# One layer of a hybrid mixer and expert kernel: loads in order of use, a first piece of three tiles, and early splits of the last head's output made sooner

## The chip, the cores and the metric

The kernel runs on one core of one Trainium2 chip, in one launch. The metric is the device time of that launch in microseconds, taken as the median of several runs. Before the change three runs gave 1456.88, 1457.09 and 1457.78 us, so the median is 1457.09 us.

## The reference

A layer with 16 meta rows ahead of 1024 tokens, so 1040 rows of width 1024, all in float32:

```
h   = concat(meta, x)                            # 1040 x 1024
xn  = rms_norm(h, mix_norm_w)
proj = xn @ w_in                                 # 28 column tiles of 128, and 8 columns for a, b
y_a = rms_norm_by_64(gate_b * conv3(gate_c * u))
q, k, v = silu(conv4(qkv)); q, k l2-normalised
o   = gated_delta_rule(q, k, v, g, beta)         # 4 heads of 128, chunks of rows
y_b = rms_norm(o) * silu(z)
h   = h + concat(y_a, y_b) @ w_out
h   = h + experts(rms_norm(h, ffn_norm_w))       # 32 experts, 2 per token
out = rms_norm(h, final_norm_w)[16:]
```

## The kernel before

**Split products.** Each float32 matrix that TensorE multiplies is split in two: a high part, which ScalarE makes by copying into a reduced format, and a low part, which VectorE makes as the value less its high part. A product is then three matmuls (high by high, high by low, low by high), the three lines 1132 to 1134 in `project` and the lines 441 to 443 in `out_product`.

**The start.** The 1040 rows are ten tiles of C = 104 rows. A tile is loaded by the SyncE queue (`load_x`, line 1086), squared, summed and turned into a scale by ScalarE (`token_norm`, lines 1390 to 1398), multiplied by that scale and by the norm weight `mixrow` on VectorE (line 1581), transposed in eight blocks by TensorE (`turn_x`, line 1157), and split (high part ScalarE line 1403, low part VectorE line 1587). The 1040 columns of `xn_hi` and `xn_lo` that result are handed to `project` in the three pieces of `PIECE`: 348, 346 and 346 columns. The first nine units of projection are three pieces by three weight tiles (Q, K, V of head 0); unit n works on piece n // 3. The weight tiles `p_raw` are loaded by the same SyncE queue (`load_p`, line 1091), split by `hi_part` (line 1374) and `lo_part` (line 1572).

The SyncE queue issues row tiles 0 to 3, then the three weight tiles, then row tiles 4 to 9. The ScalarE queue issues first the small constants, then 104 copies of the norm weight, the parameters and the rest of the constants. TensorE transposes tiles 0 to 3, then does unit 0, and one more tile's transpose ahead of each unit. ScalarE keeps tile t+2's norm ahead of tile t-1's high part. ScalarE evacuates each unit (`first_piece`, line 1384) and VectorE convolves each evacuated unit (four instructions, lines 1624 and 1622), after all low parts and after the low part of the small weight `wab` (line 1594). Then come the products with `wab` (line 1179), the projection of Z for head 0, which needs a weight tile whose low part VectorE makes after the nine convolutions, and the gates.

**The heads.** Heads 0 to 2 run in a loop, head 3 (`last`) is unrolled behind it. A head solves a triangular system in rounds: `z` (line 1254), `rz` (line 1252), and `ttr` (line 1250) on TensorE, each in three groups that go to banks 3 to 5; VectorE takes `z` (line 1691) and `rz` (line 1689) out, ScalarE `ttr` (line 1482). Projection units, called fills, are put between the rounds; in head 3 they are used up after the round rz2. Then follows a scan over ten chunks.

**The early output product.** In head 3 the output weight is split too: ScalarE `w_out_hi` (line 1525) in three parts after ttr3, ttr4 and ttr5, GpSimd `w_out_lo` (line 1878). The first three blocks of 128 rows of the output product take six of their eight weight tiles (`EARLY`) as fills of the scan. Their left operand is split by `early_high` on ScalarE (line 1488) and `early_low` on VectorE (line 1761). `early_high(0)`, `(1)`, `(2)` stand behind the three parts of the `w_out_hi` split; `early_low` stands behind rz3, rz4 and rz5 in VectorE's order. Block u's split lies where the weight slot u of the projection was: slot 1 held GC, slot 2 UU, slot 0 GB.

Of the kernel before, what the change touches and what calls it, by code (L numbers as in the profile page):

```python
# [21 lines left out]
F32 = mybir.dt.float32  # L22
I32 = mybir.dt.int32
F32R = mybir.dt.float32r
ALU = mybir.AluOpType
# [7 lines left out]
C = 104  # L33
# [5 lines left out]
PIECE = [(0, 348), (348, 346), (694, 346)]  # L39
# [72 lines left out]
def layer_kernel(nc, x, consts, par, mix_w, wt, w_out, ffn_w, fin_w, w_gate, w_up, w_down, out):  # L112
    ctx = ExitStack()
    with ctx:  # L114
# [144 lines left out]
        x_loaded = [sem(f"token_rows_loaded{s}") for s in range(NC)]  # L259
# [464 lines left out]
        def tail_vector(dve):  # L724
# [247 lines left out]
            for t in range(FT + 1):  # L972
                if t < FT:
                    dve.wait_ge(hf_loaded[t], 32)
# [107 lines left out]
        def _(sp):  # L1082
            def load_x(t):
                if t >= NX:
                    sp.wait_ge(xn_done, t - NX + 1)
                sp.dma_start(x_sb[t % NX][0:C, :], x[t * C:(t + 1) * C, :]).then_inc(x_loaded[t], 16)
# [6 lines left out]
            for t in range(4):  # L1093
                load_x(t)
            for n, s in enumerate((1, 2, 0)):
                load_p(s, n)
            for t in range(4, NC):
                load_x(t)
# [49 lines left out]
        def _(pe):  # L1148
# [216 lines left out]
        def _(act):  # L1365
            act.dma_start(const_sb[:, 0:NFIRST], consts[:, 0:NFIRST]).then_inc(s_first, 16)
            act.dma_start(mixrow[0:C, :], mix_w[0:C, :]).then_inc(s_mix, 16)
            act.dma_start(par_sb, par).then_inc(s_const, 16)
            act.dma_start(const_sb[:, NFIRST:NCONST], consts[:, NFIRST:NCONST]).then_inc(s_const, 16)
# [16 lines left out]
            def token_norm(t):  # L1386
                act.wait_ge(x_loaded[t], 16)
# [19 lines left out]
            for t in range(NC + 1):  # L1407
                for tt in (range(3) if t == 0 else range(t + 2, min(t + 3, NC))):
                    token_norm(tt)
                if t:  # L1410
                    xn_high(t - 1)
                if t in (2, 3, 4):
                    hi_part((1, 2, 0)[t - 2], 1)
                if t == 5:
                    act.wait_ge(s_const, 32)
                    nc.scalar.activation(wab_hl[:, :, 0:8], wab, ACT.Copy).then_inc(wab_done, 1)
                if t >= 6:
                    if t == 6:
                        act.wait_ge(zeros_done, 3)
                    first_piece(t - 6)  # L1420
            for n in range(5, 9):
                first_piece(n)
# [67 lines left out]
            def mixer(h, last):  # L1490
# [25 lines left out]
                for n in range(1, LEVELS - 1):  # L1516
                    grp(h, f"ttr{n}", tI)
                    if not last and n in (3, 5):
                        kind = Q if n == 3 else K
                        hi_part(SLOT[kind], use(h, kind))  # L1520
                    if last and n >= 3:
# [4 lines left out]
                        early_high(n - 3)  # L1526
# [39 lines left out]
        def _(dve):  # L1566
            for u in range(3):
# [7 lines left out]
            dve.wait_ge(s_mix, 16)  # L1575
            for t in range(NC + 1):
                if t < NC:
                    dve.wait_ge(rstd_done, t + 1)
                    if t >= NB:
                        dve.wait_ge(xt_done, 2 * (t - NB + 1))  # L1580
                    nc.vector.scalar_tensor_tensor(xn_sb[t % NB][0:C, :], x_sb[t % NX][0:C, :], nstat[0:C, 2, t:t + 1],
                                                   mixrow[0:C, :], ALU.mult, ALU.mult).then_inc(xn_done, 1)
                if t:
                    for b in range(2):
                        dve.wait_ge(xhi_done, 2 * (t - 1) + b + 1)
                        cols = slice((t - 1) * C, t * C)
                        nc.vector.tensor_tensor(xn_lo[:, 4 * b:4 * b + 4, cols],
                                                bank[3 + 2 * ((t - 1) % 2) + b][:, 0:4 * C].rearrange("p (k c) -> p k c", k=4),
                                                xn_hi[:, 4 * b:4 * b + 4, cols].bitcast(F32),
                                                ALU.subtract).then_inc(xlo_done, 1)  # L1590
                if t in (2, 3, 4):
                    lo_part((1, 2, 0)[t - 2], 1)
# [102 lines left out]
            def mixer(h, last):  # L1695
# [60 lines left out]
                def early_low(t):  # L1756
# [3 lines left out]
                    dve.wait_ge(ye_hi, t + 1)  # L1760
# [3 lines left out]
                if last:  # L1764
# [182 lines left out]
```

## Time and profile before

| what | value |
|---|---|
| median of three runs | 1457.09 us |
| the profiled execution | 1456.85 us |
| its span | 1455.0 us |
| TensorE busy | 1291.5 us, 89% |
| TensorE weight loads | 1138.4 us, 78% |
| VectorE busy | 918.7 us, 63% |
| ScalarE busy | 719.6 us, 49% |
| GpSimd busy | 162.7 us, 11% |
| mean granted TensorE clock | 0.946 |

Between the span and the time of the execution lie 1.85 us. The granted clock is a share of full speed: 1.00 is 2.4 GHz and 0.50 is 1.2 GHz; a stretch between the two was partly at each. An instruction's row gives its start and its duration; durations of matmuls overlap, so what one costs is the distance from its start to the next start. The number in brackets is how long the engine was idle ahead of the row, with what ended that.

### The profile page before, as it was taken

The numbers are of one execution on the slowest core, as the hardware profiler recorded it, in microseconds if no ns is written. First come the engines' busy times: TensorE is split into PE (matmuls) and PEld (weight loads), VectorE is DVE, ScalarE is ACT, GpSimd is POOL, SyncE is SP. The second block draws the span as 40 slices with busy tenths as digits, with TensorE's granted clock in tenths as the row PEclk, the third lists the DMA queues.
The fourth block names the chain that finished last, engine by engine and source line by source line (L and its number), as shares of the span: only waits on it lengthen the run. The fifth ranks groups of instructions, "written<-read, shape, count | busy, mean of one in ns | idle before, by whom it ended". The sixth has DMA issues, their size and how long they took to land. (4 is left out here: it accounts for less than half of the span.)

```text
span 1455.0 us, 20112 instructions
## 1 busy us (share of the span) xinstructions
PE 1291.5 (89%) x7434; PEld 1138.4 (78%) x7434; DVE 918.7 (63%) x1138; ACT 719.6 (49%) x920; POOL 162.7 (11%) x143
## 2 busy tenths in 40 slices
PE   3999998999899989789995599999999999999950
PEld 2989997999799989767885488888888888888840
DVE  4654555445445463433315688888888888888827
ACT  6251234123412341233312477777777877777723
POOL 0010111011101120420000311111111111111000
PEclk9999999999999999889995799999999999999985
DMA  7000111010001010305510799999999999999848
GB/s 201 30 30 16 30 30 30 15 30 30 30 15 30 29 30 1 116 0 201 190 60 28 271 350 369 372 373 382 382 384 378 383 377 375 378 378 374 316 175 345
DMA packets 38163, 274.01 MB, mean 188 GB/s; under 512 B 8159, under 2 KB 8415, under 8 KB 25815
## 3 DMA queue, kind: packets, MB, share of 16 engines
q1 hardware_dynamic: 28050, 250.69, 46.1%
q0 software_dynamic: 9216, 16.80, 3.0%
q10 hardware_dynamic: 837, 5.65, 1.1%
q8 instruction: 46, 0.75, 0.2%
q14 instruction: 14, 0.11, 0.0%
HBM read 260.52 MB, written 29.36 MB: 199 GB/s over the span
## 5 line engine op out<-in xcount | busy, mean ns | idle before, releaser
L787 DVE TENSOR_TENSOR w_lo<-w_raw,w_hi 128x2048 fp32r<-128x2048 f32 x192 | 433.4, 2286 | 67.7 <-ACT w_hi L642 67.7
L642 ACT ACTIVATE w_hi<-w_raw 128x2048 fp32r<-128x2048 f32 x192 | 357.1, 1916 | 18.5 <-PE bank L524 13.8
L1132 PE MATMUL bank<-xn_hi,p_hi 128*128 128x346 f32 (+1 forms) x672 | 231.9, 345 | 0.0
L1133 PE MATMUL bank<-xn_lo,p_hi 128*128 128x346 f32 (+1 forms) x672 | 219.9, 327 | 0.0
L1134 PE MATMUL bank<-xn_hi,p_lo 128*128 128x346 f32 (+1 forms) x672 | 219.1, 326 | 0.0
L522 PE MATMUL bank<-w_hi,xgT_hi 128*128 128x512 f32 x512 | 206.5, 403 | 2.9 <-DVE xgT_lo L911 2.9
L524 PE MATMUL bank<-w_hi,xgT_lo 128*128 128x512 f32 x512 | 200.8, 392 | 0.0
L523 PE MATMUL bank<-w_lo,xgT_hi 128*128 128x512 f32 x512 | 200.5, 392 | 0.0
L1132 PEld LDWEIGHTS bank<-xn_hi,p_hi 128*128 128x128 f32 x672 | 130.4, 194 | 0.4
L1133 PEld LDWEIGHTS bank<-xn_lo,p_hi 128*128 128x128 f32 x672 | 130.2, 194 | 0.3
L1134 PEld LDWEIGHTS bank<-xn_hi,p_lo 128*128 128x128 f32 x672 | 129.3, 192 | 0.0
L522 PEld LDWEIGHTS bank<-w_hi,xgT_hi 128*128 128x128 f32 x512 | 97.0, 189 | 21.6 <-issue 3.6
L524 PEld LDWEIGHTS bank<-w_hi,xgT_lo 128*128 128x128 f32 x512 | 96.7, 189 | 20.8
L523 PEld LDWEIGHTS bank<-w_lo,xgT_hi 128*128 128x128 f32 x512 | 97.1, 190 | 18.4
L1482 ACT ACTIVATE arena<-bank 104x416 f32<-104x416 f32 (+1 forms) x72 | 28.4, 459 | 158.2 <-PE bank L1250 158.1
L522 PE MATMUL bank<-w_hi,hidT_hi 128*128 128x512 f32 x256 | 100.7, 393 | 3.0 <-DVE hidT_lo L922 3.0
L524 PE MATMUL bank<-w_hi,hidT_lo 128*128 128x512 f32 x256 | 100.3, 392 | 0.0
L523 PE MATMUL bank<-w_lo,hidT_hi 128*128 128x512 f32 x256 | 100.2, 391 | 0.0
L996 POOL DMA_INDIRECT y_rows<-arena x32 | 32.2, 1006 | 504.9 <-ACT arena L673 504.9
L1822 DVE SCALAR_TENSOR_TENSOR arena<-arena,bank 128x128 f32<-128x128 f32 x40 | 13.9, 347 | 86.3 <-PE bank L1292 86.3
L673 ACT ACTIVATE arena<-bank,arena 128x512 f32<-128x512 f32 x64 | 40.5, 685 | 52.0 <-PE bank L524 52.0
L1378 ACT ACTIVATE arena<-bank 128x346 f32<-128x346 f32 (+1 forms) x39 | 18.0, 461 | 95.7 <-PE bank L1134 95.6
(233 smaller groups left out, 2050.9 us busy)
## 6 DMA issues: line engine op xcount, KB each, us to landing
w_raw<-in_w_down SPq DMA_DIRECT2D x32, 2048.0 KB, 9.8
w_raw<-in_w_gate SPq DMA_DIRECT2D x31, 2048.0 KB, 10.4
w_raw<-in_w_up SPq DMA_DIRECT2D x31, 2048.0 KB, 9.5
p_raw<-in_w_tiles SPq DMA_DIRECT2D x28, 512.0 KB, 3.6
arena<-y_rows SPq DMA_DIRECT2D x8, 1024.0 KB, 12.0
arena<-in_tokens SPq DMA_DIRECT2D x10, 416.0 KB
w_out_raw<-in_w_out SPq DMA_DIRECT2D x4, 1024.0 KB, 8.6
arena<-in_tokens SPq DMA_DIRECT2D x8, 512.0 KB, 4.2
```

Source lines behind the costliest of these rows:

```text
L522: nc.tensor.matmul(out, xh, wh, start=start, stop=False)
L523: nc.tensor.matmul(out, xh, wl, start=False, stop=False)
L524: return nc.tensor.matmul(out, xl, wh, start=False, stop=stop_)
L642: nc.scalar.activation(w_hi[m][:, half], wraw[m][:, half], ACT.Copy).then_inc(hi_done[m], 1)
L673: m = nc.scalar.activation(ysb[p][:, b * 512:(b + 1) * 512], bank[3 + b][:, :], ACT.Copy, scale=wcol[p])
L787: nc.vector.tensor_tensor(w_lo[m][:, half], wraw[m][:, half], w_hi[m][:, half].bitcast(F32), ALU.subtract).then_inc(lo_done[m], 1)
L996: nc.gpsimd.indirect_dma_start(out=y_dram, out_offset=bass.IndirectOffsetOnAxis(ap=si[p], axis=0), in_=ysb[p], in_offset=None, bounds_chec ...
L1132: nc.tensor.matmul(out[:, 0:n], p_hi[slot][:, k, :], hi, start=(k == 0), stop=False)
L1133: nc.tensor.matmul(out[:, 0:n], p_hi[slot][:, k, :], lo, start=False, stop=False)
L1134: m = nc.tensor.matmul(out[:, 0:n], p_lo[slot][:, k, :], hi, start=False, stop=(k == KD - 1))
L1378: nc.scalar.activation(raw[buf][:, 3 + o:3 + o + n], bank[pc][:, 0:n], ACT.Copy).then_inc(proj_act, 1)
L1482: nc.scalar.activation(dst[0:C, gsl(g), :], bmat(g)[0:C], ACT.Copy).then_inc(gdn_act, 1)
```

## The change

Three things are changed together.

1. **Loads.** The norm weight is loaded as one row, first on the SyncE queue; TensorE spreads it over the partitions by a product with a row of ones, and VectorE copies it out of two banks into `mixrow`. Row tiles 0 to 3 follow, then weight tile, row tile 4, weight tile, row tile 5, weight tile, row tile 6 and on. The parameters and the remaining constants come last on that queue; the ScalarE queue only issues the small constants. Row loads share eight semaphores.
2. **Pieces.** `PIECE` is 312, 364 and 364 columns, so piece 0 needs three row tiles, piece 1 seven and piece 2 ten. TensorE transposes tiles 0 to 2, then tile 3 ahead of unit 0, tile 4 ahead of unit 1, tiles 5 and 6 ahead of unit 2, and 7, 8, 9 ahead of units 3, 4, 5. ScalarE and VectorE are reordered to match; the split of `wab` now stands behind the evacuation of unit 5.
3. **Last head.** `early_high(1)` moves behind ttr1, `early_high(2)` and `(0)` behind ttr2, `early_low(1)` behind rz2, `early_low(2)` and `(0)` behind rz3.

```diff
-PIECE = [(0, 348), (348, 346), (694, 346)]
+PIECE = [(0, 3 * C), (3 * C, 364), (3 * C + 364, 364)]
+READY = [-(-(o + n) // C) for o, n in PIECE]
@@ sync
-            for t in range(4):
-                load_x(t)
-            for n, s in enumerate((1, 2, 0)):
-                load_p(s, n)
-            for t in range(4, NC):
-                load_x(t)
+            sp.dma_start(xn_sb[NB - 1][0:1, :], mix_w[0:1, :]).then_inc(s_mix, 16)
+            for t in range(NC):
+                load_x(t)
+                if t in (3, 4, 5):
+                    load_p((1, 2, 0)[t - 3], t - 3)
+            sp.dma_start(par_sb, par).then_inc(s_const, 16)
+            sp.dma_start(const_sb[:, NFIRST:NCONST], consts[:, NFIRST:NCONST]).then_inc(s_const, 16)
@@ tensor
-            for t in range(4):
+            pe.wait_ge(s_mix, 16)
+            pe.wait_ge(mix_one, 1)
+            for b in range(2):
+                nc.tensor.matmul(bank[b][0:C, 0:512], r_sb[0:1, 0:C], xn_sb[NB - 1][0:1, b * 512:(b + 1) * 512],
+                                 start=True, stop=True).then_inc(mix_ps, 1)
+            for t in range(3):
                 turn_x(t)
             for n in range(9):
                 pc, s = n // 3, n % 3
-                if n + 4 < NC:
-                    turn_x(n + 4)
-                pe.wait_ge(xlo_done, 2 * (4, 7, 10)[pc])
+                for t in ((3,), (4,), (5, 6), (7,), (8,), (9,))[n] if n < 6 else ():
+                    turn_x(t)
+                pe.wait_ge(xlo_done, 2 * READY[pc])
@@ early_unit
-                if k == 0 and b == 0:
-                    pe.wait_ge(ye_lo, t + 1)
+                if n == 0:
+                    pe.wait_ge(ye_lo, 3)
@@ scalar
-            for t in range(NC + 1):
...
+            for t in range(3):
+                token_norm(t)
+            for t in range(NC):
+                xn_high(t)
+                if t == 0:
+                    hi_part(1, 1)
+                if t == 2:
+                    token_norm(3)
+                    hi_part(2, 1)
+                if t >= 2 and t + 2 < NC:
+                    token_norm(t + 2)
+                if t == 3:
+                    hi_part(0, 1)
+                    act.wait_ge(zeros_done, 3)
+                if t >= 4:
+                    first_piece(t - 4)
+            act.wait_ge(s_const, 32)
+            nc.scalar.activation(wab_hl[:, :, 0:8], wab, ACT.Copy).then_inc(wab_done, 1)
+            for n in range(6, 9):
                 first_piece(n)
@@ scalar, mixer
+                    if last and n == 1:
+                        early_high(1)
+                    if last and n == 2:
+                        act.wait_ge(proj_done, tile_done(h, GB))
+                        early_high(2)
+                        early_high(0)
...
-                        early_high(n - 3)
@@ vector (scale and low part in ScalarE's order)
+            for t in range(3):
+                token_scale(t)
+            for t in range(NC):
+                xn_low(t)
+                if t == 0:
+                    lo_part(1, 1)
+                if t == 2:
+                    token_scale(3)
+                    lo_part(2, 1)
+                if t >= 2 and t + 2 < NC:
+                    token_scale(t + 2)
+                if t == 3:
+                    lo_part(0, 1)
@@ vector, mixer
                     grp(h, "rz2")
+                    early_low(1)
                     mix_conv()
...
                         grp(h, f"rz{n}")
-                        early_low(n - 3)
+                        if n == 3:
+                            early_low(2)
+                            early_low(0)
...
-                    if last and n == 5:
-                        early_low(2)
```

## Rows read from the trace of the kernel before

**Rows 1.** First part of the page: busy time of each engine.
```profile
PE 1291.5 (89%) x7434; PEld 1138.4 (78%) x7434; DVE 918.7 (63%) x1138; ACT 719.6 (49%) x920; POOL 162.7 (11%) x143
```

**Rows 2.** Timeline, 0 to 35: start, duration (us), instruction, [idle before, releaser].
```profile
5.08 1.06 ACT L1390 ACTIVATE arena<-arena 104x1024 f32<-104x1024 f32 x1 [0.83 <-DMA arena<-in_tokens]
6.66 0.20 ACT L1398 ACTIVATE arena<-arena 104x1 f32<-104x1 f32 x1
10.07 2.48 DVE L1581 SCALAR_TENSOR_TENSOR arena<-arena 104x1024 f32<-104x1024 f32 x2 [9.15 <-DMA arena<-in_mix_w]
...
17.14 1.09 DVE L1587 TENSOR_TENSOR xn_lo<-bank,xn_hi 128x416 fp32r<-128x416 f32 x2 [4.59 <-ACT xn_hi L1403]
21.76 1.06 ACT L1390 ACTIVATE arena<-arena 104x1024 f32<-104x1024 f32 x1 [4.25 <-DMA arena<-in_tokens]
24.17 1.06 ACT L1374 ACTIVATE p_hi<-p_raw 128x1024 fp32r<-128x1024 f32 x1
31.09 1.65 PE L1157 MATMUL bank<-arena 104*128 104x104 f32 x8 [1.71 <-DVE arena L1581]
32.43 0.64 PE L1132 MATMUL bank<-xn_hi,p_hi 128*128 128x348 f32 x1
```

**Rows 3.** Windows: stretch, length, engines' busy time, granted clock, DMA share, GB/s.
```profile
15.00:19.00 4.00, 0.00 (x0) 0.00 (x0) 1.86 (x3) 2.45 (x6) 0.00 (x0) 1.00 0.83 339
20.00:30.00 10.00, 2.77 (x15) 2.13 (x13) 5.83 (x8) 8.05 (x18) 0.00 (x0) 1.00 0.84 204
```

**Rows 4.** Timeline, 58 to 80, the end of the first nine units.
```profile
58.54 0.17 DVE L1612 COPY arena<-arena 128x16 f32<-128x16 f32 x1
61.06 0.46 ACT L1384 ACTIVATE arena<-bank 128x346 f32<-128x346 f32 x1 [2.92 <-PE bank L1134]
64.86 0.46 ACT L1384 ACTIVATE arena<-bank 128x346 f32<-128x346 f32 x1 [3.34 <-PE bank L1134]
76.46 1.81 DVE L1622 SCALAR_TENSOR_TENSOR arena<-arena 128x346 f32<-128x346 f32 x3
78.19 1.22 DVE L1572 TENSOR_TENSOR p_lo<-p_raw,p_hi 128x1024 fp32r<-128x1024 f32 x1
79.88 0.32 PE L1132 MATMUL bank<-xn_hi,p_hi 128*128 128x348 f32 x1
```

**Rows 5.** Timeline of TensorE at the start of head 1.
```profile
238.30 3.83 PE L1234 MATMUL bank<-arena 104*128 104x416 f32 x6 [4.61 <-issue]
```

**Rows 6.** TensorE behind an idle stretch (timeline), and three windows with their granted clock.
```profile
551.39 3.58 PE L1254 MATMUL bank<-arena 104*104 104x104 f32 x20 [1.95 <-ACT arena L1482]
311.00:323.00 12.00, 11.86 (x110) 10.66 (x108) 7.02 (x13) 7.15 (x12) 4.52 (x2) 1.00 0.16 45
551.00:555.00 4.00, 3.61 (x21) 3.61 (x22) 1.43 (x3) 0.98 (x3) 0.00 (x0) 0.58 0.00 0
603.70:609.70 6.00, 5.95 (x34) 5.95 (x35) 2.33 (x5) 1.25 (x4) 1.71 (x1) 0.50 0.14 53
```

**Rows 7.** Timeline of the last head's rounds.
```profile
592.50 0.52 DVE L1743 TENSOR_TENSOR arena<-bank,arena 128x346 f32<-128x346 f32 x1 [2.79 <-PE bank L1134]
595.34 2.00 PE L1252 MATMUL bank<-arena 104*104 104x104 f32 x20
596.27 1.60 DVE L1689 TENSOR_TENSOR arena<-arena,bank 104x416 f32<-104x416 f32 x3 [0.23 <-PE bank L1252]
601.66 1.53 DVE L1761 TENSOR_TENSOR y_lo<-arena,y_hi 128x768 fp32r<-128x768 f32 x1 [3.78 <-ACT y_hi L1488]
603.75 3.80 PE L1252 MATMUL bank<-arena 104*104 104x104 f32 x20 [3.37 <-DVE arena L1691]
613.32 2.89 DVE L1761 TENSOR_TENSOR y_lo<-arena,y_hi 128x768 fp32r<-128x768 f32 x1 [5.36 <-ACT y_hi L1488]
616.77 3.80 PE L1252 MATMUL bank<-arena 104*104 104x104 f32 x20 [5.40 <-DVE arena L1691]
629.80 3.50 PE L1252 MATMUL bank<-arena 104*104 104x104 f32 x20 [3.32 <-DVE arena L1691]
```

More of the change, by code:

```diff
@@ L38 @@
 Z, GC, UU, GB, Q, K, V = range(KINDS)
-PIECE = [(0, 348), (348, 346), (694, 346)]
+PIECE = [(0, 3 * C), (3 * C, 364), (3 * C + 364, 364)]
+READY = [-(-(o + n) // C) for o, n in PIECE]
+NXS = 8
 LEVELS = 7
@@ L258, in layer_kernel @@
         s_wout = [sem(f"w_out_loaded{i}") for i in range(4)]
-        x_loaded = [sem(f"token_rows_loaded{s}") for s in range(NC)]
+        x_loaded = [sem(f"token_rows_loaded{s}") for s in range(NXS)]
+        mix_one, mix_ps, mix_done = sem("mix_ones_set"), sem("mix_in_psum"), sem("mix_rows_done")
         s_mix, wab_done, abt_done = sem("mix_row_loaded"), sem("wab_done"), sem("abt_done")
@@ L973, in tail_vector @@
                 if t < FT:
-                    dve.wait_ge(hf_loaded[t], 32)
+                    dve.wait_ge(hf_loaded[t], 48 if t + NXS < NC else 32)
                     dve.wait_ge(yf_loaded[t], 16)
@@ L1085, in load_x @@
                     sp.wait_ge(xn_done, t - NX + 1)
-                sp.dma_start(x_sb[t % NX][0:C, :], x[t * C:(t + 1) * C, :]).then_inc(x_loaded[t], 16)
+                sp.dma_start(x_sb[t % NX][0:C, :], x[t * C:(t + 1) * C, :]).then_inc(x_loaded[t % NXS], 16)
             def load_p(s, n):
@@ L1366, in _ @@
             act.dma_start(const_sb[:, 0:NFIRST], consts[:, 0:NFIRST]).then_inc(s_first, 16)
-            act.dma_start(mixrow[0:C, :], mix_w[0:C, :]).then_inc(s_mix, 16)
-            act.dma_start(par_sb, par).then_inc(s_const, 16)
-            act.dma_start(const_sb[:, NFIRST:NCONST], consts[:, NFIRST:NCONST]).then_inc(s_const, 16)
             nc.scalar.preload_act_table_set("natural_log_exp_and_others")
@@ L1386, in token_norm @@
             def token_norm(t):
-                act.wait_ge(x_loaded[t], 16)
+                act.wait_ge(x_loaded[t % NXS], (t // NXS + 1) * 16)
                 if t:
@@ L1405, in xn_high @@
                                          ACT.Copy).then_inc(xhi_done, 1)
-            for t in range(NC + 1):
[L1408 to L1421, printed above, removed]
+            for t in range(3):
[17 more added lines that the diff above has]
+            for n in range(6, 9):
                 first_piece(n)
@@ L1566, in _ @@
         def _(dve):
+            nc.vector.memset(r_sb[0:1, :], 1.0).then_inc(mix_one, 1)
             for u in range(3):
@@ L1573, in lo_part @@
                                         ALU.subtract).then_inc(p_lo_done[slot], 1)
[L1575 to L1592, printed above, removed]
@@ new lines, in _, with token_scale @@
+            for b in range(2):
+                dve.wait_ge(mix_ps, b + 1)
+                nc.vector.tensor_copy(mixrow[0:C, b * 512:(b + 1) * 512], bank[b][0:C, 0:512]).then_inc(mix_done, 1)
+            dve.wait_ge(mix_done, 2)
+            def token_scale(t):
+                dve.wait_ge(rstd_done, t + 1)
+                if t >= NB:
+                    dve.wait_ge(xt_done, 2 * (t - NB + 1))
+                nc.vector.scalar_tensor_tensor(xn_sb[t % NB][0:C, :], x_sb[t % NX][0:C, :], nstat[0:C, 2, t:t + 1],
+                                               mixrow[0:C, :], ALU.mult, ALU.mult).then_inc(xn_done, 1)
@@ new lines, in xn_low @@
+            def xn_low(t):
+                cols = slice(t * C, (t + 1) * C)
+                for b in range(2):
+                    dve.wait_ge(xhi_done, 2 * t + b + 1)
+                    nc.vector.tensor_tensor(xn_lo[:, 4 * b:4 * b + 4, cols],
+                                            bank[3 + 2 * (t % 2) + b][:, 0:4 * C].rearrange("p (k c) -> p k c", k=4),
+                                            xn_hi[:, 4 * b:4 * b + 4, cols].bitcast(F32), ALU.subtract).then_inc(xlo_done, 1)
+            for t in range(3):
+                token_scale(t)
@@ L1759, in early_low @@
                             for a in (y_lo[t], yT[:, :, META + t * 128:META + (t + 1) * 128], y_hi[t].bitcast(F32))]
-                    dve.wait_ge(ye_hi, t + 1)
+                    dve.wait_ge(ye_hi, (3, 1, 2)[t])
                     nc.vector.tensor_tensor(part[0], part[1], part[2], ALU.subtract).then_inc(ye_lo, 1)
```

## The prediction

> **What bounds the kernel now.** I read the page's first part first: TensorE is busy for 89% of the span [rows 1], so time can come only from stretches where it waits, or runs at the lower of its two clock levels. The timeline shows the reader the first such stretch. TensorE's steady work starts with the transposes of tile 3 at 31.09 and unit 0 at 32.43. Ahead of it ScalarE sits idle for 4.25 us, until row tile 4 is there at 21.76, because three weight tiles stand before that tile in the queue, and it takes up the first weight tile only at 24.17; VectorE waits until 10.07 for the norm weight [rows 2]. Windows say what the loads can give: 339 GB/s while weight tiles move, 204 GB/s with row tiles alone [rows 3]. The timeline from 58 to 80 shows who comes next: VectorE convolves without a pause from 58.71 to 78.27 and ends the low part of the Z tile at 79.41, and TensorE takes it at 79.88 [rows 4]. So VectorE has 0.5 us of slack there. Last, the rounds of the last head: TensorE waits 3.37, 5.40 and 3.32 us at `rz4`, `rz5` and `rz6` for VectorE's `z` evacuation, and VectorE itself had stood behind `early_low`, which waited 3.78 and 5.36 us for ScalarE [rows 7]. Each wait is followed by a round at the lower clock: `rz` takes 3.80, 3.80 and 3.50 us there, against 2.00 before [rows 7].
>
> **Part 1, the loads.** A row tile of 426 KB takes 2.08 us at 204 GB/s, a weight tile of 524 KB takes 1.55 us at 339 GB/s [rows 3]. Tile 0 is used at 5.08 [rows 2], and as the norm weight's 426 KB and the parameters no longer run beside it, I leave it there. Then tiles 1 to 3 are usable at 7.2, 9.2 and 11.3, the first weight tile at 12.9, tile 4 at 15.0, and with two more weight tiles between, tile 9 at 28.5. The parameters and constants (0.94 MB) end near 32, and their first users are the splits of `wab` near 50. They cost nothing. SyncE's queue waits for freed buffers only at tiles 7 to 9, of which the first three scalings, done near 13.6, are the condition.
>
> The norm weight now needs two 512-column products. The nearest row is 3.83 us for 1040 columns at the lower clock [rows 5], so 3.8 us; with small constants there at about 5.3 and a copy of 0.6 (an estimate from 1.09 for two of 416 [rows 2]) it is ready near 9.8, where it was 10.07. Its bounds are 7.5 (upper clock) and 10.5; both lie hidden, as the next step waits for the weight tile.
>
> The chain on ScalarE, with 1.78 for a norm (5.08 to 6.86), 1.24 for a scaling, 1.65 for a tile's transposes, about 1.0 for its high part and 1.06 for a weight's [rows 2]: norms 0 to 2 end at 11.0; tile 0 is scaled at 11.1, turned at 12.8, its high part ends at 13.3, the weight's at 14.3, tile 1's at 15.2. Tile 2's transposes need tile 0's low part (14.6), so its high part ends at 16.9, norm 3 at 18.6, scaling 3 at 19.9. Piece 0 would be ready near 18, but tile 3's transposes stand ahead of unit 0 in TensorE's order; they start at 20.0, where they started at 31.09. That is 11.1 us earlier, and from there TensorE has the same list in sum (the same transposes, the same 1040 columns), with tile 9 in place long before piece 2 needs it.
>
> So the `wab` products would end at 68.8 instead of 79.9. **What is late next** is VectorE. Its convolutions used to start as soon as the last low part was done, ahead of unit 5's end (ScalarE evacuates it at 61.06 [rows 4]). Now the `wab` split stands behind that evacuation on ScalarE, and VectorE waits for it, with all nine convolutions queued behind the wait and the Z tile's low part behind those. Unit 5 ends at 60.95 less 11.1, less 0.6 for 18 columns that went from pieces 0 and 1 to piece 2 (72 matmuls at 0.458 ns a column, from 3.80 us for a unit [rows 4]): 49.3. Evacuation and the small splits bring 50.6, and the chain from 58.71 to 79.41 is 20.7 us long [rows 4], so Z starts at 71.3. The gain is 79.88 - 71.3 = 8.6 us, and a wait of 2.5 us is new. TensorE pays for such a wait with the clock: behind 1.95 us of idle the window shows 0.58 over 4 us, and behind the wait at `rz4` 0.50 over 6 us; at that level a round takes 3.80 for 2.00, so a stretch of 6 us loses 2.9 [rows 6, 7]. I take 2.9 (bounds 0 and 4). **Part 1: -8.6 + 2.9 = -5.7 us.**
>
> A rule of the Trainium skill ("DMA: Bandwidth & Descriptors", Why a DMA increments its semaphore by 16) says that a transfer is spread over the largest number of engines up to 16 that divides its partitions. For 104 that is 13; the DMA share of 0.84 with row tiles alone [rows 3] agrees. Were it not so, at 339 GB/s the first weight tile would be there at 9.6 instead of 12.9, and part 1 would gain some 3 us more. My sum goes by the row.
>
> **Part 2, the pieces in the heads.** Each of 28 column tiles is still 1040 columns. The new price is unseen for 312 and 364 columns. If a matmul costs by column, the sum is unchanged. If 312 columns cost as much as 346 (0.158), it is 28 x 24 x 0.0155 = 10.4 us more. An `rz` of 20 matmuls takes 2.00 us [rows 7], 0.10 each with its weight load, so nothing holds a step above 0.14, and I take the price by column. A shorter Z piece 0 lets ScalarE's chain at a head's end begin 0.37 us earlier, a longer piece 2 gives 0.17 back: -0.2 at each of three borders, bounds 0 and -1.5. **Part 2: -0.6 us.**
>
> **Part 3, the last head.** The moved instructions are three high parts and three low parts, nothing is added. `early_low(1)` goes ahead of the mix convolution, where VectorE later idles 2.79 us before the last GB piece [rows 7]: free. Without that cover it would cost 0.9. `early_high(1)`, `(2)` and `(0)` fall into ScalarE's idle time ahead of `ttr2` and `ttr3`; its new wait for the GB fills is met at about 592.3, and what is queued behind it is the `ttr3` evacuation, near 597.7. `early_low(2)` and `(0)` now stand between `rz3` (ends 597.87) and `z4`. Their price: 1.53 and 2.89 us in the rows, but a weight's low part of 1024 elements takes 1.22 alone [rows 4], so 768 should take 0.93, and the rows beyond that lie beside GpSimd's `w_out_lo`. With 0.93 each VectorE is free at 599.7, TensorE's `z4` (behind `rz3` at 595.34 [rows 7] and `ttr3`) has its first group then, and `rz4` starts near 600.5 instead of 603.75: -3.2. With 1.53 each it is 601.7: -2.0. The waits at `rz5` and `rz6` go whole: -5.4 and -3.3. Together -11.9 us. Next in line is ScalarE: `ttr5` stands behind three `w_out_hi` copies, which end just in time by this reckoning.
>
> Three low-clock stretches follow the three waits at 2.9 each (3.80 for 2.00, and the scan's first chunk). Without the waits, do they go? From 311 to 323 an earlier head does the same rounds with no fills, and the window shows 11.86 of 12 us busy and 1.00 granted [rows 6]. I take all three as gone: -8.6. **Part 3: -20.5 us.** GpSimd's last low parts end near 620 then, and the scan asks for the sixth at about 622.
>
> On VectorE and GpSimd: the Trainium skill ("GPSIMD Engine Reference", Specifications) says that the two share SBUF interfaces and contend when a VectorE instruction has two SBUF inputs. The 2.89 us against 0.93 bears that out [rows 4, 7]. By the rule `early_low` in its new place, ahead of the weight split, is cheap; by the 1.53 of the row alone 1.2 us less would be gained.
>
> **Sum.** 1456.85 - 5.7 - 0.6 - 20.5 = 1430.05; the median stands 0.24 above the profiled execution, so 1430.3 us.
>
> **Rivals.**
> (a) The low clock stays in the unfilled rounds, which now last 20 us without a pause instead of 12. For it: TensorE's small matmuls leave it at 0.50 for all of 603.7 to 609.7 though it is busy [rows 6]. Against: the 1.00 from 311 to 323. Only the waits go: 1430.3 + 8.6 = 1438.9; with one stretch left 1433.2.
> (b) The start is bound by loads. If a row tile amid weight tiles takes its 2.08 us and completions come 3 us later than reckoned, `hi_part` of the first weight holds ScalarE, and all behind it: 1433.3. Against: 339 GB/s when both kinds are queued.
> (c) The floor of part 2: 1430.3 + 10.4 = 1440.7.
> (d) Slower than before: the new wait ahead of Z drops TensorE to its lower level, and it stays there through head 0's start. Each us at that level costs 0.47; the gains of 26.8 are used up from 57 us on, that is, if it lasted from 71 to 128. From 71 through the first scan's half it would give 1460. Against: no stretch in the rows is longer than about 7 us.
>
> **How the numbers follow.** Forecast 0.48 (own range 1427 to 1433.5), (a) with one stretch 0.17, (a) in full 0.12, (b) 0.12, (c) 0.06, (d) 0.03, and 0.02 for parts that cancel otherwise. The range 1425 to 1441 leaves out (d), the end of (c), and a start with no clock loss beside loads faster than the rows. Faster (by over 0.2%, some 3 us, about what can be told from no change) has all but (d) and the rest: 0.95; same 0.02, slower 0.03.
>
> **What would show it.** Tile 3's transposes near 20 and unit 0 near 21.6; the convolutions starting near 50.6 behind the `wab` split; a TensorE wait of 2 to 3 us ahead of Z near 71, then a granted clock near 0.5; `early_low` at 0.9 us; no wait over 0.5 us at `rz4` to `rz6`, `rz` at 2.0 us, and the scan some 27 us earlier than before. Wrong would be a first unit later than 24, `rz` rows still at 3.8, or units of piece 0 above 3.6 us.

## The result, and the profile after

The changed kernel takes 1422.48 us (median of four runs, 1421.91 to 1424.46), against 1457.43 us for the kernel before beside it. The ratio is 0.9763, with a 95% interval of 0.9744 to 0.9782: 35 us faster. I had forecast 1430.3 us and a range from 1425 to 1441, so the direction was right and the gain was larger than the range allows.

The spans of the two profiled executions are 1455.0 and 1420.6 us. To place the 34.4 us I take marks that both traces have: VectorE's clearing of the state, one per head, the first residual of the last scan, and the last scaling of the head's output.

| stretch | before | after | difference |
|---|---|---|---|
| start to head 0's mark | 91.64 | 83.24 | -8.40 |
| head 0 | 144.97 | 143.02 | -1.95 |
| heads 1 and 2 | 293.97 | 293.26 | -0.71 |
| head 3, mark to its z3 on VectorE | 63.86 | 60.57 | -3.29 |
| head 3, z3 to the scan's first residual | 40.29 | 20.49 | -19.80 |
| head 3, scan and output | 39.85 | 38.75 | -1.10 |
| the rest | 780.42 | 781.27 | +0.85 |

The start, in the timeline of the changed kernel (columns as in [rows 2]):

```profile
5.30 1.06 ACT L1396 ACTIVATE arena<-arena 104x1024 f32<-104x1024 f32 x1 [2.87 <-DMA arena<-in_tokens]
8.00 2.60 DVE L1600 SCALAR_TENSOR_TENSOR arena<-arena 104x1024 f32<-104x1024 f32 x2
13.48 1.06 ACT L1380 ACTIVATE p_hi<-p_raw 128x1024 fp32r<-128x1024 f32 x1 [1.17 <-DMA p_raw<-in_w_tiles]
19.14 1.65 PE L1161 MATMUL bank<-arena 104*128 104x104 f32 x8 [3.56 <-DVE arena L1600]
20.48 0.61 PE L1136 MATMUL bank<-xn_hi,p_hi 128*128 128x312 f32 x1
...
49.17 0.23 DVE L1625 TENSOR_TENSOR wab_hl<-arena,wab_hl 128x64 fp32r<-128x64 f32 x1 [3.38 <-ACT wab_hl L1430]
70.21 0.41 PE L1136 MATMUL bank<-xn_hi,p_hi 128*128 128x312 f32 x1 [2.31 <-DVE p_lo L1588]
```

Before the change unit 0 started at 32.43, now it starts at 20.48. Tile 3 is turned at 19.14. The row at 31.09, which the prediction took for tile 3, is tile 4: the kernel before turned tile 4 too ahead of unit 0, and its timeline has tile 3 at 27.74:

```profile
27.74 1.65 PE L1157 MATMUL bank<-arena 104*128 104x104 f32 x8 [6.62 <-DVE arena L1581]
```

VectorE sits idle for 3.38 us until ScalarE has made the high part of the small weight `wab`, takes its low part at 49.17 and only then convolves, and TensorE waits 2.31 us for the Z tile's low part. Z starts at 70.21, 9.67 us earlier than before [rows 4]. The windows of the changed kernel (columns as in [rows 3]) show the clock behind that wait, and in the last head:

```profile
71.00:75.00 4.00, 4.00 (x20) 4.00 (x19) 0.00 (x0) 1.43 (x2) 0.00 (x0) 0.63 0.00 0
525.00:545.00 20.00, 15.86 (x132) 15.30 (x131) 15.30 (x24) 6.16 (x11) 2.40 (x2) 1.00 0.06 24
```

In the last head the kernel before had two stretches at the lower clock, one behind a pause ahead of the products `gq` and one behind the pause ahead of `z1`, at 551 to 555 [rows 6]. Here is the first, in the timeline and the window of that kernel:

```profile
540.10 1.07 PE L1243 MATMUL bank<-arena 128*104 128x104 f32 x9 [2.39 <-DVE arena L1682]
```

```profile
542.00:546.00 4.00, 4.00 (x25) 4.00 (x24) 3.40 (x8) 0.00 (x0) 0.00 (x0) 0.64 0.00 0
```

The last head's rounds in the timeline of the changed kernel, the answers to [rows 7]:

```profile
570.58 0.95 DVE L1792 TENSOR_TENSOR y_lo<-arena,y_hi 128x768 fp32r<-128x768 f32 x1
583.44 1.82 DVE L1792 TENSOR_TENSOR y_lo<-arena,y_hi 128x768 fp32r<-128x768 f32 x2
585.86 2.03 PE L1261 MATMUL bank<-arena 104*104 104x104 f32 x20
590.78 2.00 PE L1261 MATMUL bank<-arena 104*104 104x104 f32 x20
597.27 2.00 PE L1261 MATMUL bank<-arena 104*104 104x104 f32 x20
600.08 0.47 PE L1284 MATMUL bank<-arena 128*104 128x128 f32 x2 [0.81 <-ACT arena L1446]
```

No `rz` has a wait in brackets any more, each takes 2.0 us, and `early_low` takes 0.95 and 0.91. The scan's new last wait is 0.81 us for ScalarE's norm.

### The profile page after: what moved, and what is told of

Same layout as the page of the kernel before. It is cut to its first block and busy times, and to the rows that moved or that the text cites. A ratio compares the mean times of both kernels' runs of the same rounds, so it can differ in the third digit from the quotient of the medians.

```text
span 1420.6 us, 20123 instructions
## 1 busy us (share of the span) xinstructions
PE 1281.9 (90%) x7438; PEld 1125.2 (79%) x7438; DVE 915.8 (64%) x1141; ACT 719.6 (51%) x920; POOL 160.6 (11%) x143
## 5 line engine op out<-in xcount | busy, mean ns | idle before, releaser
L1136 PE MATMUL bank<-xn_hi,p_hi 128*128 128x364 f32 (+1 forms) x672 | 231.8, 345 | 2.3 <-DVE p_lo L1588 2.3
L1138 PE MATMUL bank<-xn_hi,p_lo 128*128 128x364 f32 (+1 forms) x672 | 219.3, 326 | 0.0
L1137 PE MATMUL bank<-xn_lo,p_hi 128*128 128x364 f32 (+1 forms) x672 | 218.8, 326 | 0.0
L1722 DVE TENSOR_TENSOR arena<-bank,arena 104x416 f32<-104x416 f32 (+1 forms) x72 | 35.4, 517 | 49.4 <-PE bank L1263 46.3
## 6 DMA issues: line engine op xcount, KB each, us to landing
arena<-y_rows SPq DMA_DIRECT2D x8, 1024.0 KB, 11.9
```

Source lines behind the costliest of these rows:

```text
L1136: nc.tensor.matmul(out[:, 0:n], p_hi[slot][:, k, :], hi, start=(k == 0), stop=False)
L1137: nc.tensor.matmul(out[:, 0:n], p_hi[slot][:, k, :], lo, start=False, stop=False)
L1138: m = nc.tensor.matmul(out[:, 0:n], p_lo[slot][:, k, :], hi, start=False, stop=(k == KD - 1))
L1722: m = nc.vector.tensor_tensor(zz[0:C, s], bmat(g)[0:C], lev[:, int(name[1:]), :].unsqueeze(1).to_broadcast([C, n, C]), ALU.mult)
```

## The experiments

Two theories stood at first. **A**: each part pays at its own place, by its own waits. **B**: part of the gain comes from the clock, which falls or stays behind a pause depending on the moment of the pause. Each kernel has one profiled execution, while its time is a median of 4 to 25. To compare, I sum the time at the lower clock between 60 and 720 us, from windows of 5 us (one less the granted clock, doubled, times 5): 57.9 us before, 27.3 us after.

Profiles of the same instructions differ in this too. The kernel with part 3 alone has the code of the kernel before up to the last head, and there its profile takes 143.52 us for head 0 and 291.37 us for heads 1 and 2, against 144.97 and 293.97. So a difference of some 2 us in one stretch of two profiles shows no effect of an edit by itself.

**Part 3 alone, on the kernel before.**

```diff
+                    if last and n == 1:
+                        early_high(1)
...
-                        early_low(n - 3)
+                        if n == 3:
+                            early_low(2)
+                            early_low(0)
```

> The kernel before with part 3 alone (early splits moved). Theory A, each part pays where it stands: the rounds of the last head lose their three waits and the low-clock stretches behind them, z3 to the first scan chunk takes 20.5 us instead of 40.3, and the time is 1457.4 - 20.9 = 1436.5 us. Theory B, part of the gain of the whole change came from pauses meeting the clock gate at another moment: the stretches at 0.5 granted clock that stand at 540 to 560 in the kernel before (some 3 us lost) stay here, as nothing ahead of them moves, so the last head up to z3 still takes 63.9 us; the whole is again near 1436.5. Both agree on the sum; if the head up to z3 takes 60.6 us here too, theory B falls and the moved splits themselves saved it.

Measured 1435.93 us, ratio 0.9848 (0.9815 to 0.9881). The three waits went here as in the full change (20.49 us from z3 to the first residual), and the two low-clock stretches ahead of z3 stayed; the second is even twice as long, so the head takes 65.39 us up to z3 where 63.9 was expected. Two windows of this kernel show them:

```profile
536.00:541.00 5.00, 5.00 (x36) 5.00 (x35) 3.53 (x9) 0.00 (x0) 0.00 (x0) 0.66 0.00 0
546.00:555.00 9.00, 7.96 (x39) 7.96 (x40) 3.58 (x5) 1.63 (x4) 0.00 (x0) 0.62 0.00 0
```

So the moved splits give 21.2 us and did not save the 3.3 us ahead of z3.

**Parts 1 and 2 alone** (the changed kernel with the splits put back).

```diff
-                    if last and n == 1:
-                        early_high(1)
...
+                        early_high(n - 3)
...
-                        if n == 3:
-                            early_low(2)
-                            early_low(0)
+                        early_low(n - 3)
```

> The changed kernel with the last head's splits put back to where they were: parts 1 and 2 alone. Theory A: the start and head 0 give 9.9 us and the other heads 0.7, so 1457.4 - 10.6 + 0.9 = 1447.7 us, and the last head takes its 144 us as before. Theory B: as this kernel reaches the last head 11 us earlier, like the changed one, its pause ahead of z1 and that at gq meet the gate as in the changed kernel: no stretch at 0.5 between the head's start and z3, the head up to z3 takes 60.6 us, and the time is 1444.5 us.

Measured 1442.42 us, ratio 0.9901 (0.9871 to 0.9930), 15 us faster. The last head's stretches ahead of z3 are gone (60.56 us up to z3, and a granted clock of 1.00 from 520 to 580), so what removed them is in parts 1 and 2. 21.2 and 14.7 us add to 35.9, near the 35 us of both.

**Pieces alone.**

```diff
-PIECE = [(0, 348), (348, 346), (694, 346)]
+PIECE = [(0, 3 * C), (3 * C, 364), (3 * C + 364, 364)]
...
-                pe.wait_ge(xlo_done, 2 * (4, 7, 10)[pc])
+                pe.wait_ge(xlo_done, 2 * (3, 7, 10)[pc])
```

> The kernel before with the pieces 312, 364, 364 and piece 0 asking for three row tiles, loads and order as before (tiles 0 to 3 are still turned ahead of unit 0). My prediction: matmuls cost by column, so heads are 0.2 us shorter each and the time is 1456.8 us. Rival, a floor under a matmul's step of 0.158 us: 1467 us, with units of piece 0 at 3.80 us. Theory B adds that the low-clock stretches may come out otherwise by up to 3 us either way though nothing else moves.

Measured 1451.08 us, ratio 0.9963 (0.9952 to 0.9975). The floor falls: a 312-column matmul steps by 0.144 us, in proportion to the 0.158 of 346 columns. But the sizes alone gave 6.1 us (3.6 to 7.0 by the interval) where I had 0.6. Head 0's mark is at 91.62, so the start gained nothing. The last head is 3.3 us shorter up to z3, without its two stretches (a granted clock of 1.00 from 535 to 555), and the time at the lower clock fell from 57.9 to 47.8 us, at 0.47 us lost per us some 4.8 us. Heads 1 and 2 are 1.2 us shorter and head 0 1.9 us, which is within what two profiles of the same instructions differ by.

**The small weight's split sooner, on the changed kernel.**

```diff
+                if t == 9:
+                    act.wait_ge(s_const, 32)
+                    nc.scalar.activation(wab_hl[:, :, 0:8], wab, ACT.Copy).then_inc(wab_done, 1)
                 if t >= 4:
                     first_piece(t - 4)
```

> The changed kernel with the small weight's split put ahead of the evacuation of unit 5 on ScalarE, as soon as the last tile's high part is made. If the 2.3 us TensorE wait ahead of Z is the convolution chain that starts too late (my step on VectorE), that chain starts at 46.2 instead of 49.5, the wait goes and the low-clock stretch behind it (70 to 75, mean 0.66) with it: 2.3 + 1.3 = 3.6 us faster, 1418.9 us. By theory B the stretch only moves to the gate products after Z, where the kernel before had it: 2.3 us less 1.5, 1421.7 us. If it is something else that holds Z, no change.

Measured 1416.55 us, ratio 0.9732 (0.9700 to 0.9764), 5.9 us faster than the changed kernel. The timeline has the split at 46.42, and TensorE comes to Z without a wait; the window over it shows the clock:

```profile
64.00:76.00 12.00, 11.42 (x85) 9.12 (x83) 4.43 (x12) 6.86 (x13) 0.09 (x1) 1.00 0.01 4
```

The start is 3.40 us shorter, as expected, and head 0 has lost its stretch too (1.6 us), which was not; the pause ahead of it is 1.92 us against 1.93, so that loss is not shown to come from the edit. The convolutions were what held Z.

**The changed kernel, later by a delay.** One memset ahead of the first load, 2048 elements (1.76 us) or 4096 (3.47 us).

```diff
+            nc.vector.memset(arena[:, zy.end - 8320:zy.end - 8320 + 2048], 0.0).then_inc(late_start, 1)
...
+            sp.wait_ge(late_start, 1)
             sp.dma_start(xn_sb[NB - 1][0:1, :], mix_w[0:1, :]).then_inc(s_mix, 16)
```

> The changed kernel with one VectorE memset of 2048 elements per partition that the first load waits for; nothing else differs, so all work starts later by that memset, about 1.5 us (its length is in the trace). If the low-clock stretches follow from what TensorE does alone, each stretch comes after the same pause and is as long as in the changed kernel, and the time is 1422.5 + 1.5 = 1424.0 us. Theory B, that it matters when a pause falls: stretches appear, go or change length, and the time less the delay is off by 1 to 5 us.

> The same with 4096 elements, about 3 us later. Activity alone: 1425.5 us and the same stretches. Theory B: other stretches than in the changed kernel and than with the shorter delay, the time less the delay off by 1 to 5 us, most likely upward, since the changed kernel's last head had none.

Measured 1424.24 and 1426.74 us. Tile 3 is turned 2.21 and 3.48 us later, and the times are 1.8 and 4.3 us longer. The wait ahead of Z is 2.31 us in both, as in the changed kernel. Behind it the short delay has no stretch at the lower clock, and the long one has two (lower clock in all 23.9 and 30.6 us). So the same pause with the same instructions around it does not always bring the clock down; whether the delay does this, or one execution differs so from the next, these two single profiles do not tell. The time less the delay moved by under 1 us, and the last head had no stretch ahead of z3 in either.

**Bytes back on ScalarE's queue**, on the changed kernel.

```diff
+            act.dma_start(mixrow[0:C, :], mix_w[0:C, :]).then_inc(s_mix, 16)
+            act.dma_start(par_sb, par).then_inc(s_const, 16)
+            act.dma_start(const_sb[:, NFIRST:NCONST], consts[:, NFIRST:NCONST]).then_inc(s_const, 16)
...
-            for b in range(2):
-                dve.wait_ge(mix_ps, b + 1)
...
-            dve.wait_ge(mix_done, 2)
+            dve.wait_ge(s_mix, 16)
```

> The changed kernel with the 104 copies of the norm weight, the parameters and the constants back on ScalarE's queue ahead of all, and no broadcast; row and weight tiles in the new order. By my reckoning row tiles come 2.9 to 3.7 us apart again as in the kernel before, the first weight tile near 17 instead of 13.5, so tile 3 is turned near 22.5 instead of 19.1 and the time is 3.4 us longer, 1425.9 us. Rival: the order of the queue did it all, and the bytes are hidden: 1422.5 us.

Measured 1426.32 us, 3.8 us slower than the changed kernel. The bytes are not hidden. The timeline has the first weight tile taken up at 16.75 and tile 3 turned at 22.41, as reckoned:

```profile
16.75 1.06 ACT L1375 ACTIVATE p_hi<-p_raw 128x1024 fp32r<-128x1024 f32 x1 [3.03 <-DMA p_raw<-in_w_tiles]
22.41 1.65 PE L1158 MATMUL bank<-arena 104*128 104x104 f32 x8 [5.41 <-DVE arena L1591]
```

**The queue's order alone**, on the kernel before.

```diff
-            for t in range(4):
+            for t in range(NC):
                 load_x(t)
-            for n, s in enumerate((1, 2, 0)):
-                load_p(s, n)
-            for t in range(4, NC):
-                load_x(t)
+                if t in (3, 4, 5):
+                    load_p((1, 2, 0)[t - 3], t - 3)
```

> The kernel before with only the SyncE queue reordered: row tiles 0 to 3, weight, tile 4, weight, tile 5, weight, tiles 6 to 9. ScalarE takes tile 4's norm ahead of tile 2's high part in that kernel, and waited for it until 21.76. Tile 4 then comes 3 us sooner (two weight tiles less at 1.55 each), near 18.7, and the first unit near 29.3 instead of 32.4: 1457.2 - 3.0 = 1454.2 us, with up to 3 us either way from the clock. Rival: the chain of ScalarE and VectorE holds the first unit anyway, 1457.2 us.

Measured 1454.61 us, ratio 0.9981 (0.9962 to 1.0000), 2.7 us, hardly clear of no change; unit 0 starts at 30.45 (29.3 expected), and head 0's mark is 2.75 us earlier. So of the 8.4 us up to that mark the order gives some 2.7, the bytes 3.2 (86.45 against 83.24), each read from two profiles and on different kernels. That the rest comes from the three-tile piece with its reordered chain is not shown, as I did not run it by itself.

**Pieces of 312, 382 and 346**, on the kernel before.

```diff
-PIECE = [(0, 348), (348, 346), (694, 346)]
+PIECE = [(0, 3 * C), (3 * C, 382), (694, 346)]
...
-                pe.wait_ge(xlo_done, 2 * (4, 7, 10)[pc])
+                pe.wait_ge(xlo_done, 2 * (3, 7, 10)[pc])
```

> The kernel before with pieces of 312, 382 and 346 columns: piece 0 as changed, piece 2 as it was. In all six kernels run so far with piece 2 at 364 columns the last head has no low-clock stretch ahead of z3, in the three with 346 it has two. Theory C, the fill of piece 2 between grow and vtr decides: with 346 the pause at gq is 2.4 us again, the clock falls behind it and behind the pause at z1, the last head is 3.2 us longer than with 312, 364, 364, and the time is 1451.1 + 3.2 = 1454.3 us. Rival, piece 0 decides (the short fill ahead of ttr0): no stretch there and 1451.1 us. Rival, chance of the moment: neither is told by it.

Measured 1452.03 us, ratio 0.9975 (0.9963 to 0.9987), no stretch ahead of z3. Theory C falls: piece 2 need not change for the stretches to go. The rival fits, though piece 1 changed here too. The timeline and the window of this kernel say more:

```profile
534.64 0.70 PE L1243 MATMUL bank<-arena 128*104 128x104 f32 x5 [2.42 <-DVE arena L1682]
```

```profile
535.00:545.00 10.00, 8.07 (x73) 7.69 (x72) 8.31 (x16) 3.37 (x6) 0.00 (x0) 1.00 0.01 2
```

The pause is 2.42 us and the clock stays; in the kernel before it was 2.39 us and the clock fell. (It is the pause of the row at 540.10 above.) The pause's length by itself does not decide.

**`ttr0` ahead of the weights' high parts**, in every head, on the kernel with the sooner split.

```diff
+                grp(h, "ttr0", rT)
                 hi_part(2, use(h, UU))
                 hi_part(0, use(h, GB))
-                grp(h, "ttr0", rT)
```

> The changed kernel with the sooner wab split (1416.6 us) and, in every head, ScalarE's evacuation of ttr0 ahead of the two weight high parts for UU and GB that stood before it. The 1.95 us pause of TensorE at z1 is that evacuation standing behind two copies of 1.0 us. It should go in all four heads, 7.8 us; three heads have a low-clock stretch behind it, 1.6 us each, and if these are set by the pause they go too: 1416.6 - 7.8 - 4.8 = 1404.0 us. If the clock falls all the same: 1408.8 us. If the weight parts, now later, hold VectorE's z1 evacuation and so rz1: no gain, 1416.6 us.

Measured 1409.28 us, ratio 0.9682 (0.9664 to 0.9699): the fastest of all, 13.2 us better than the changed kernel. The pause at z1 is gone in all four heads. Against the kernel with the sooner split alone it gives 7.3 us, 5.3 less than the 1404.0 forecast. Heads 1 and 2 gave 3.5 and 3.9 us, the pause and the stretch behind it. But new stretches came, 6.8 us between 70 and 80 and one in the last head, so that 1409.28 lies near the 1408.8 of "the clock falls all the same" by another way. The one in the last head, in the timeline and the window, follows a pause of 2.21 us, which in the changed kernel (2.22 us) had none behind it:

```profile
515.26 0.70 PE L1252 MATMUL bank<-arena 128*104 128x104 f32 x5 [2.21 <-DVE arena L1714]
```

```profile
516.50:520.50 4.00, 4.00 (x26) 4.00 (x25) 3.25 (x8) 0.00 (x0) 0.00 (x0) 0.57 0.00 0
```

**Unit 0 ahead of tile 3**, on the kernel with the sooner split.

```diff
-                for t in ((3,), (4,), (5, 6), (7,), (8,), (9,))[n] if n < 6 else ():
+                for t in ((), (3, 4), (5, 6), (7,), (8,), (9,))[n] if n < 6 else ():
```

> The changed kernel with the sooner wab split, and unit 0 ahead of tile 3's transposes, which then stand with tile 4's ahead of unit 1. My prediction held that tile 3's transposes kept piece 0 waiting from 18 to 20: unit 0 should start near 18 instead of 20.4, all nine units end some 2 us sooner, 1414.5 us. Rival: ScalarE's chain (tile 3's high part, then norms 5 and 6) moves back by as much and takes the gain at unit 2 or 3: 1416.6 us.

Measured 1419.71 us, 3.2 us slower than without. Unit 0 does start at 17.58, but TensorE then waits at a later tile's transposes:

```profile
17.58 0.63 PE L1136 MATMUL bank<-xn_hi,p_hi 128*128 128x312 f32 x1 [2.01 <-DVE xn_lo L1608]
31.35 0.93 PE L1161 MATMUL bank<-arena 104*128 104x104 f32 x8 [2.04 <-DVE arena L1601]
```

The rival holds: the chain of ScalarE and VectorE, not TensorE's order, sets the pace there. Of the 2.4 us between the two profiles head 0's mark is 0.76 us and one more low-clock stretch in head 0 is 1.6 us. Part of the 0.76 is the clock as well: TensorE's steps keep the length of the lower level for the first 5.4 us of unit 0, against 2.8 us without the edit.

**`early_low(2)` and `(0)` behind rz4**, on the changed kernel.

```diff
-                        if n == 3:
+                        if n == 4:
                             early_low(2)
                             early_low(0)
```

> The changed kernel with early_low(2) and (0) one round pair later, behind rz4, where GpSimd makes w_out_lo. If the two engines share what both need, as the 2.89 us rows before hinted, these two take 1.5 to 2.9 us each instead of 0.93, VectorE's z5 is 3.5 to 5 us late, and a low-clock stretch follows: 1422.5 + 4 + 2 = 1428.5 us. Rival, the length is not GpSimd's doing: 0.93 each, z5 as late as z4 is now, 1422.5 to 1423.5 us.

Measured 1428.68 us, 6.2 us slower than the changed kernel. VectorE and GpSimd in the timeline of this kernel, one row for each instruction:

```profile
587.32 2.38 POOL L1910 TENSOR_TENSOR w_out_lo<-w_out_raw,w_out_hi 128x1024 fp32r<-128x1024 f32 x1
587.63 2.88 DVE L1792 TENSOR_TENSOR y_lo<-arena,y_hi 128x768 fp32r<-128x768 f32 x1
589.86 2.85 POOL L1910 TENSOR_TENSOR w_out_lo<-w_out_raw,w_out_hi 128x1024 fp32r<-128x1024 f32 x1 [0.17 <-ACT w_out_hi L1541]
590.43 3.10 DVE L1792 TENSOR_TENSOR y_lo<-arena,y_hi 128x768 fp32r<-128x768 f32 x1
592.67 3.08 POOL L1910 TENSOR_TENSOR w_out_lo<-w_out_raw,w_out_hi 128x1024 fp32r<-128x1024 f32 x1
```

Two low parts take 5.91 us beside GpSimd and 1.82 us without it. GpSimd's take 2.85 and 3.08 us where they start beside a running one of VectorE, and 2.38 where they do not (4.70 us for two in the changed kernel). The Trainium skill ("SBUF — State Buffer", SBUF: two separate sides) calls the pair an exclusive lock held for a whole instruction, also for a VectorE instruction with two SBUF inputs against a GpSimd one that reads SBUF. This run agrees: the rows take turns. VectorE's first starts at 587.63 and ends 0.81 us behind the end of GpSimd's at 589.70, its second starts at 590.43 and ends 0.82 us behind GpSimd's end at 592.71, and both remainders are near the 0.91 us that it takes alone. GpSimd's second ends 2.20 us behind VectorE's end at 590.51, its third 2.22 us behind 593.53, near its own 2.35. VectorE's rounds, which read PSUM and SBUF, keep their 1.36 us beside GpSimd.

**The kernel before, later by a delay** of 0.91, 1.76 and 2.62 us (memsets of 1024, 2048 and 3072 elements ahead of both queues' first loads).

```diff
+            act.wait_ge(late_start, 1)
             act.dma_start(const_sb[:, 0:NFIRST], consts[:, 0:NFIRST]).then_inc(s_first, 16)
```

> The kernel before, with one VectorE memset of 1024 elements ahead of the first loads of both queues: the same instructions with the same pauses, all about 1.2 us later. Theory B, the moment decides: at least one of the three delays (1024, 2048, 3072 elements) brings the kernel without the two stretches at the lower clock ahead of z3 in the last head (then 60.6 us from the head's start to z3 in place of 63.9), though the 2.39 us and 1.95 us pauses are unchanged; and the time less the delay moves by 1.5 to 6 us up or down among the three. Rival, the pauses' length and what stands before them decide: the same stretches in all three, and 1457 us plus the delay each.

> The same with 2048 elements, about 2.2 us later. Theory B: other stretches than with 1024 or 3072 elements, time less delay anywhere from 1451 to 1460 us. Rival: 1459.3 us and the stretches of the kernel before.

> The same with 3072 elements, about 3 us later. Theory B: time less delay anywhere from 1451 to 1460 us. Rival: 1460 us and the stretches of the kernel before.

Measured 1458.66, 1459.70 and 1460.75 us beside 1456.97: +1.7, +2.7 and +3.8 us, 0.8 to 1.2 us more than the delays. The two stretches ahead of z3 are in all three profiles, behind the same pauses. So in the last head the moment since the launch does not decide either, and there theory B falls. What goes with the stretches is the piece sizes: with the old sizes all six profiled kernels have them, with a 312-column piece 0 ten of eleven have none. That this works through what TensorE did before the pause is likely and not shown, and which part of it counts is open. Ahead of the last head chance plays a part: single executions of one kernel differ, 25 of the kernel before lie from 1452.19 to 1460.93 us. The clock goes with this: the six executions with a mean granted clock of 0.944 took 1459.95 to 1460.93 us, the two with 0.950 took 1452.19 and 1454.70.

## Why the prediction was wrong

Right in sign, in the waits and in the loads; the steps that failed are two terms for the clock, one too dear and one left out. On the spans 26.8 us were forecast and 34.4 measured.

- **Part 1, the loads and the chain: right, with one misread row and some luck.** Tile 3 was turned at 19.14 (forecast 20.0), convolutions started at 49.5 (50.6), the wait ahead of Z was 2.31 us (2.5), Z at 70.21 (71.3). This is 1.1 us more than forecast. But the row at 31.09, from which the 11.1 us are counted, is tile 4's, so TensorE had not "the same list in sum" from there: the changed kernel has one tile's transposes more, 0.66 us each at the upper clock (25.03 to 25.69 in its timeline). Yet from 31.09 to the end of the `wab` products it was 48.8 us before, and from 19.14 it is 48.8 us now. What made up for it was not in the prediction: the matmuls of unit 0 stepped by 0.29 us for 348 columns during 3.9 us before, and by 0.26 us for 312 during only 2.2 us now. A window shows 1.00 there in both, because the trace has no record of the clock ahead of its first rise, at 36.3 and 22.7. The kernel with part 3 alone, with the start unchanged, has 2.2 us of this too, so it differs from one execution to the next, and the sum came out by luck. The broadcast was cheaper than my 9.8: the norm weight was in use at 8.00, hidden as I had it. Row tiles came 2.2 us apart (norms at 5.30, 7.57 and 9.79), near the 2.08 that 204 GB/s gave. The Trainium skill's rule on engines per transfer ("DMA: Bandwidth & Descriptors", Why a DMA increments its semaphore by 16) gives 13 of 16 for 104 partitions. The share of 0.84 is near that, but the window with weight tiles, which have 128 partitions, shows 0.83 as well [rows 3], so the share does not show the rule.
- **Part 1, the clock's price: the first step that failed.** I added 2.9 us for a low-clock stretch behind the new wait. It came (0.63 from 71 to 75) and cost 1.3 us, Z to head 0's mark taking 13.03 us for 11.76. I had taken the price from the 6 us behind the wait at `rz4`, while my own row behind 1.95 us of idle (0.58 over 4 us) gives 0.42 x 2 x 4 x 0.47 = 1.6. Besides, the profile before has a stretch of its own right behind, at 85 to 95, and the profile after has none there: head 0's mark to its first residual is 84.30 us for 85.78. The net is -0.2, 3.1 us of the miss. I had counted the stretch that comes and not asked what becomes of the one that was there. Of the 3.1 us, 1.6 are the price. The other 1.5 are not shown to come from the change, as the kernel with part 3 alone, whose start is the old one, lacks that stretch too (84.34 us).
- **Part 2, the pieces: the second.** -0.6 us forecast. The last head lost two low-clock stretches ahead of z3, 3.3 us, which I had not in the sum: I weighed the price of a matmul, and put the clock's part at nothing. The runs with the pieces alone and with 312, 382 and 346 columns show that the sizes took the two stretches away; how, stays open. Heads 1 and 2 gave 0.7 together and head 0 some 0.5, no more than profiles of the same instructions differ by. The bound I gave, -1.5, was worked from durations at one level alone.
- **Part 3: right.** -19.80 - 1.10 = -20.9 us, for -20.5. Of the waits 12.1 us went and 0.81 came, 11.3 for my 11.9, which leaves 9.6 for the clock where I had 8.6. The run with part 3 alone gave 21.2 us, and `early_low` cost 0.93 as taken from the weight's low part, not the 1.53 and 2.89 of its own rows.
- **The rivals.** (a), the clock staying low in unfilled rounds, fell: `rz` takes 2.00 throughout. (b) fell by the landing times, the first weight tile being taken up at 13.48 (12.9 forecast). (c) fell in the run with the pieces alone. (d) had a true beginning, the wait and the lower clock, and ended after some 3 us.
- **The range** ended at 1425 because I let clock terms vary only upward from a forecast that already took all the last head's. A cheaper stretch in the start, one less behind it and two less in the last head stood outside it.

## What to carry to other kernels

A pause of some 2 us on TensorE may cost nothing more than itself, or another 1.6 us at the lower clock, or twice that. It pays to take pauses away, and a forecast of the clock's part should count the stretches that may go as well as those that come, to both sides of the sum. A term of one or two stretches should be read from many executions, as two profiles of the same instructions can differ by that much. When loads or pieces are reordered, look for what else hangs on the evacuation that moved: here a copy of 64 elements per partition held nineteen microseconds of convolutions, and one moved line gave 5.9 us. VectorE work with both inputs in SBUF belongs where GpSimd is idle.

## What the runs showed that I had not expected

- The granted clock falls behind a pause of 2.39 us in one kernel and stays behind one of 2.42 us in another; it stays behind 2.22 us and falls behind 2.21 us.
- Three piece sizes with the same sum of columns moved the whole by 6.1 us, and by the profiles most of it through the clock: 57.9 us at the lower level against 47.8.
- A window shows a granted clock of 1.00 at the start while TensorE steps at the lower level, 0.29 us for 348 columns from 32.43 to 36.31 in the kernel before, against 0.159 later: the record of the clock begins only with the first rise. There the steps have to be read.
- A VectorE instruction with two SBUF inputs took 0.91 us alone and 2.95 us beside GpSimd, each waiting for the other's instruction to end.
